# Scores of two attention heads: one fp32 product replaced by three rounded products of split queries and keys

## The reference

```python
k = rmsnorm_2(k_s, k_norm).transpose(0, 2, 1, 3)
c = jnp.cumsum(jax.nn.log_sigmoid(f_logit), axis=1).transpose(0, 2, 1)
q = rmsnorm_2(qg[..., :d].reshape(bsz, s_len, N_HEADS, HEAD_DIM), q_norm[j])
# for each block i of 128 queries:
s = jnp.einsum('bhqd,bhkd->bhqk', q_i, k, preferred_element_type=jnp.float32) * scale
s = s + c_i[..., None] - c[:, :, None, :]
s = jnp.where(kpos[None, :] <= qpos[:, None], s, -jnp.inf)
p = jax.nn.softmax(s, axis=-1)
o = jnp.einsum('bhqk,bhkd->bhqd', p.astype(v.dtype), v)
o = o * jax.nn.sigmoid(qg[..., d:])
```

## Time and profile before

| | us |
|---|---|
| median of three runs | 2042.83 |
| the three runs | 2042.83, 2043.99, 2040.23 |
| the profiled execution | 2045.83 |
| its span | 2044.0 |
| TensorE busy in the span | 2034.4 |
| VectorE, GpSimd, ScalarE busy | 963.3, 854.3, 783.7 |

### The profile page before, as it was taken

How to read it: one execution, slowest core, us unless ns; L and a number is a source line. 1 busy time by engine, 2 the same in 40 slices (tenths; PEclk the granted TensorE clock), 3 DMA queues, 4 the chain that set the end, 5 groups by cost and what they waited for, 6 DMA issues and landing times.

```text
span 2044.0 us, 24465 instructions
## 1 busy us (share of the span) xinstructions
PE 2034.4 (100%) x9826; PEld 1662.7 (81%) x9826; DVE 963.3 (47%) x1481; ACT 783.7 (38%) x1123; POOL 854.3 (42%) x357
## 2 busy tenths in 40 slices
PE   9999999999999999999999999999999999999999
PEld 7888888788888888888888888888867778888887
DVE  4588878633221314434463342444356656325242
ACT  6445656534222224512432232246256643222222
POOL 4334333544444444444444444453412234444444
PEclk9999999999999999999999999999999999999999
DMA  5222222342323222322333233232311122322333
GB/s 178 84 82 74 77 88 73 124 148 93 103 93 98 94 98 93 103 93 93 96 92 104 92 102 103 91 117 83 103 53 52 54 81 93 103 93 93 103 93 114
DMA packets 55121, 194.31 MB, mean 95 GB/s; under 512 B 6112, under 2 KB 6368, under 8 KB 55008
## 3 DMA queue, kind: packets, MB, share of 16 engines
q1 hardware_dynamic: 55008, 192.75, 29.2%
HBM read 190.62 MB, written 2.10 MB: 94 GB/s over the span
## 4 chain that ended last, share of the span: by engine, by line
PE 97%; issue 1%; DVE 1%; POOL 1%; ACT 0%; POOLq 0%; DVEq 0%
PE ps L1312 29%; PE ps L1314 29%; PE ps L1313 29%; PE ps L1626 1%; PE ps L1659 1%; PE ps L1650 1%; PE ps L1589 1%; PE ps L1591 1%; PE ps L1590 1%; PE ps L1439 1%; PE ps L1320 1%; PE ps L1341 1%; POOL w_lo L346 1%; PE ps L1366 0%; PE ps L1461 0%
## 5 line engine op out<-in xcount | busy, mean ns | idle before, releaser
L346 POOL TENSOR_TENSOR w_lo<-w_raw,w_hi 128x1024 fp32r<-128x1024 f32 x353 | 854.1, 2422 | 1177.8 <-ACT w_hi L365 1166.1
L1312 PE MATMUL ps<-a_hi,w_hi 128*128 128x512 f32 x1472 | 582.0, 395 | 1.6 <-POOL w_lo L346 1.3
L1314 PE MATMUL ps<-a_hi,w_lo 128*128 128x512 f32 x1472 | 573.9, 390 | 0.0
L1313 PE MATMUL ps<-a_lo,w_hi 128*128 128x512 f32 x1472 | 573.8, 390 | 0.0
L365 ACT CAST w_hi<-w_raw 128x1024 fp32r<-128x1024 f32 x353 | 366.2, 1041 | 324.7 <-PE ps L1314 294.4
L1312 PE MATMUL ps<-b_hi,w_hi 128*128 128x512 f32 x1176 | 459.3, 391 | 0.2 <-DVE x L787 0.2
L1314 PE MATMUL ps<-b_hi,w_lo 128*128 128x512 f32 x1176 | 457.6, 389 | 0.0
L1313 PE MATMUL ps<-b_lo,w_hi 128*128 128x512 f32 x1176 | 457.6, 389 | 0.0
L757 DVE TENSOR_TENSOR arena<-ps,inv_rms 128x512 f32<-128x512 f32 x200 | 138.0, 690 | 443.9 <-PE ps L1314 424.2
L1312 PEld LDWEIGHTS ps<-a_hi,w_hi 128*128 128x128 f32 x1472 | 276.8, 188 | 63.3 <-issue 3.2
L1313 PEld LDWEIGHTS ps<-a_lo,w_hi 128*128 128x128 f32 x1472 | 276.7, 188 | 58.6 <-issue 2.4
(11 more groups left out here) (195 smaller groups left out, 1592.9 us busy)
## 6 DMA issues: line engine op xcount, KB each, us to landing
w_raw<-in_panels SPq DMA_DIRECT2D x353, 512.0 KB, 3.5
x<-in_xT SPq DMA_DIRECT2D x16, 256.0 KB, 2.8
outT<-x SPq DMA_DIRECT2D x8, 256.0 KB, 2.0
consts<-in_const SPq DMA_DIRECT2D x1, 528.5 KB, 7.6
arena<-in_rows SPq DMA_DIRECT2D x1, 256.0 KB, 4.6
arena<-in_ws SPq DMA_DIRECT2D x1, 256.0 KB, 5.1
consts<-in_late SPq DMA_DIRECT2D x1, 168.0 KB, 2.6
params<-in_param SPq DMA_DIRECT2D x1, 116.0 KB, 2.1
```

The source lines that it names most:

```text
L346: nc.gpsimd.tensor_tensor(w_lo[:, p % RING, :], w_raw[:, p % RING, :], w_hi[:, p % RING, :].bitcast(F), ALU.subtract).then_inc(w_low, 1)
L1312: nc.tensor.matmul(o, wh, hi[:, kt, :], start=(kt == 0), stop=False)
L1313: nc.tensor.matmul(o, wh, lo[:, kt, :], start=False, stop=False)
L1314: ins = nc.tensor.matmul(o, wl, hi[:, kt, :], start=False, stop=(kt == tiles - 1))
```

## The change

The score product of a pair is no longer one fp32 product per head and block but three rounded ones: rounded query by rounded key, rounded query by rest of key, rest of query by rounded key. For this, keys and queries are split: ScalarE writes the rounded part, VectorE the rest. The split keys of pair `m` stand in tile `m` of `b_hi` and `b_lo`, where the output of the same pair will be written later; the split query stands in `sq_hi` and `sq_lo`. ScalarE splits the key of the next pair right behind the exponentials and the query behind the copies of probabilities; VectorE makes the rest of the key behind `scale_prob(a, 0)`, that of the query behind `norm_q`. Ahead of the loop both are done once for the first pair, when the last product of values has been made. `score_heads` waits for `k_low` and `q_low` instead of `q_normed`.

```diff
+        k_hi, k_lo, q_hi, q_lo = b_hi, b_lo, sq_hi, sq_lo
...
+            def split_k(a):
+                split(k_hi[:, a, :], k_all[:, a, :]).then_inc(k_high, 1)
+
+            def split_q(m):
+                act.wait_ge(q_normed, m + 1)
+                split(q_hi, q_n[:, :]).then_inc(q_high, 1)
+
+            act.wait_ge(k_normed, DT)
+            act.wait_ge(made, AT["v", DT - 1] + 1)
+            split_q(0)
+            split_k(0)
...
                 if a is not None and m is not None:
+                    split_k(m)
                     high(p + FEED)
...
                     copy_prob(a)
+                    if m is not None:
+                        split_q(m)
...
+            def rest_of_k(a):
+                dve.wait_ge(k_high, a + 1)
+                v.tensor_tensor(k_lo[:, a, :], k_all[:, a, :], k_hi[:, a, :].bitcast(F), ALU.subtract).then_inc(k_low, 1)
+
+            def rest_of_q(m):
+                dve.wait_ge(q_high, m + 1)
+                v.tensor_tensor(q_lo, q_n[:, :], q_hi.bitcast(F), ALU.subtract).then_inc(q_low, 1)
...
             take_values(1)
+            rest_of_q(0)
+            rest_of_k(0)
...
                 if a is not None and m is not None:
+                    rest_of_k(m)
                     scale_out(q_raw[:, :], p).then_inc(evicted, 1)
...
                         norm_q(m)
+                        rest_of_q(m)
                     scale_out(gate[:, m % 2, :], AT["qg", 2 * m + 1]).then_inc(evicted, 1)
...
-                pe.wait_ge(q_normed, a + 1)
+                pe.wait_ge(k_low, a + 1)
+                pe.wait_ge(q_low, a + 1)
...
-                    for side in range(2):
-                        bk, at = SCORES[side, b]
-                        nc.tensor.matmul(ps[:, bk, at:at + P * (b + 1)], q_n[half_of(side), b * P:(b + 1) * P],
-                                         k_all[half_of(side), a, 0:P * (b + 1)], start=True, stop=False)
+                    for q_part, k_part in ((q_hi, k_hi), (q_hi, k_lo), (q_lo, k_hi)):
+                        for side in range(2):
+                            bk, at = SCORES[side, b]
+                            nc.tensor.matmul(ps[:, bk, at:at + P * (b + 1)], q_part[half_of(side), b * P:(b + 1) * P],
+                                             k_part[half_of(side), a, 0:P * (b + 1)],
+                                             start=(q_part is q_hi and k_part is k_hi), stop=False)
```

More of the change, by code:

```diff
@@ L261, in build @@
         halves_made, sq_high, sq_low = sem("halves_made"), sem("sq_high"), sem("sq_low")
+        k_high, k_low, q_high, q_low = sem("k_high"), sem("k_low"), sem("q_high"), sem("q_low")
         q_squared, q_normed, gate_log, gate_arg, gate_done = (sem(n) for n in (
```

## The result

| | before | after |
|---|---|---|
| median of 19 runs each, us | 2040.37 | 2045.42 |
| most runs lie in, us | 2039.8 to 2041.0, some to 2044.0 | 2044.35 to 2045.91 |
| profiled execution, us | 2045.83 | 2044.8 |
| its span, us | 2044.0 | 2043.0 |

One run of after, at 2246.63 us with a mean granted clock of 0.851, lies apart from the other 18 and does not enter the ratio. That ratio is 1.002, interval 1.0014 to 1.0026: the change costs 2.9 to 5.3 us (the medians lie 5.05 apart). The profiled executions alone show the opposite sign, 1.0 us less after.

The account below looks back on a forecast made before the run. TensorE, with 97% of the chain, was taken to bound the kernel. First pair 0.8, middle pairs 1.0 and last pair -0.2 gave +1.6 us, forecast 2044.4 against the three-run median 2042.83; range 2038.5 to 2050.

Parts of the forecast that it names:

- first pair: First pair of heads: later weight cast and splits make TensorE wait and `low_sq` end later, +0.8 us (bounds +0.5, +1.2).
- last pair: Last pair of heads: no splits, only shorter scores, part of them lost in waits for `scale_prob`, -0.2 us.
- TensorE's saving: Score blocks of each pair: three rounded products instead of one fp32 product save 0.25 us a pair.
- Rival 3: Score blocks: weight loads are exposed, so the change isn't cheaper on TensorE; 8 x 0.9 us, 2050 us; chance 5%.
- Middle pairs: Six middle pairs: the key's split delays cast and `low_sq`, so TensorE waits; +0.17 us a pair, +1.0 us.
- One sign: Middle pairs: TensorE idle 0.3 to 0.5 us before its square sums, released by `low_sq`, would show the forecast right.
- Rival 1: Middle pairs: GpSimd's second tensor comes before `low_sq`, TensorE waits and the clock falls; 2078 us, 2060 without lower clock; 13%.
- how the profiled execution stands to the median: Base of the forecast: the profiled 2045.83 us lies 3.0 above the three-run median 2042.83, so 2047.4 becomes 2044.4.
- The start: Before the first pair's scores: splits delay the GpSimd tensor, the first key's rest ends late, TensorE waits 0.6 us.
- Rival 2: TensorE's saving comes through, 2041.9 us; second half, `low_sq` before GpSimd's second tensor in the first pair, 2037; 14% together.

Follow-up runs that it names:

- key_later: Changed kernel with the next pair's key split behind the weight cast, its rest made behind the query's norm: median 2041.32 us, ratio 0.9994 to the kernel before.
- split_twice: Changed kernel with the rounded part of the next key written twice in front of the weight cast: one execution took 2072.33 us.
- a_cast_later: Changed kernel with the pair's second weight cast only behind the split of the query: median 2042.34 us, ratio 1.0009 to the kernel before.

## Why the prediction was right, and where it was not

The time, 2045.42 us, lies in the range and 1.0 us from the forecast of 2044.4, and the change is slower, as forecast. But the change itself was forecast at +1.6 us, and the medians moved by 5.05. The close total is luck, two errors that met: the base of 2042.83, the median of three runs of which two were in the upper group, is 2.46 us above the median of 19, and the sum was 3.45 us too small. Of these, 2.25 are the first pair with its later start, 0.2 the last pair, and 1.0 lie in no trace. By the prediction's own measure of 4.1 us for what can be told from no change, the result lies on the border between "same" (72%) and "slower" (21%).

*TensorE's saving:* forecast 0.25 us a pair, measured 0.26. The blocks were forecast at 0.89, 0.59, 0.40 and 0.42 and came to 0.89, 0.58, 0.34 and 0.41. In no block is a load of 0.11 us shown except at 128 keys: the loads hide under running products on the same rows. This is against the rule that the prediction quotes from the Trainium skill, "TensorE: Matmul & The Clock Gate", section "Part 3: Packing small matmuls", that a load overlaps running products only on another row group. Rival 3 is out.

*Middle pairs:* forecast +0.17 us, measured 19.89 against 19.71 and 19.72. The split stands 0.52 us before the cast (forecast 0.54), the margin between `low_sq` and GpSimd's second tensor is 0.15 (forecast 0.13), `low_sq` keeps its turn. `key_later` and `split_twice` show the cause from both sides. One sign was off: I had named 0.3 to 0.5 us of idle time before the square sums, and 0.16 is shown. The other 0.24 us of the 0.40 lost lie in the first product behind the gap.

*Rival 1* did not happen in the middle pairs, but `split_twice` shows that it stood half a microsecond away, and its price: 24.2 us a pair where I had put 25.4. The clock was at 0.50 for 3.3 us there and for 6.7 in the traced execution of before (1498.9 to 1505.6), so the lower clock cost 1.6 us a pair, half of the 3.1 that I took.

*Last pair:* forecast -0.2, measured nothing. From its scores to the end of the program both forms take 416.2 us; the last transposes of the pair end 10.9 us after its scores begin in both. In the chain of after they stand behind `scale_prob`, so the shorter scores end in that wait, which I had put at a part only.

*First pair:* here the sum failed. I put +0.8 us, counted from the 25.62 us of the earlier trace rows, and then added it to the median of three runs. Against that form the first pair became 2.9 us shorter (22.72), since the clock did not fall in it; with the 0.8 us of the later start this is -2.1. Against the usual form, 20.57, it is +2.15 and +0.9, 3.05 where the sum has 0.8. I had seen that the profiled execution of before lay 3.0 us above the median and did not ask why. The step that failed is "how the profiled execution stands to the median": the 3 us were not an offset common to all runs, they were part of the very wait on which the term rested (5.0 us between the two traces). The start itself was right: a wait of 0.6 forecast, 0.62 measured; `low_sq` over at 1500.4 forecast, at 1500.25 measured. Held was the fourth part of `scale_prob`, not the third.

*Rival 2's* second half, in which VectorE keeps its turn in the first pair, did not occur in after, but it is how the kernel before runs in most executions, if its groups are the two forms (48 of 71). What it would have given after is shown by `a_cast_later`: 2.1 us in the first pair.

What stays open: by what the turn is decided where the distances are the same to 0.01 us, how often each form comes on a given occasion, and why the clock falls in one execution with 2.8 us of idle time and not in another with 3.0.

## What to carry to other kernels

Where a wait in a trace hangs on which of two engines gets its turn, read the trace of a second execution before a term is built on it; above all when the profiled one is off the median. And take the base from more than three runs. Cheaper products on the bounding engine give nothing if their preparation is put in front of the step that this engine waits for next: place it behind, in the idle time of its engines. And if two engines exclude each other, move the work that is not urgent (here a weight panel that is wanted a pair later) out of the other's path; on the changed kernel it gave back 2.1 us in the first pair, more than the 1.3 us that the three rounded products bring. On the kernel before no run was left in the upper group, but between the medians no gain is shown (ratio 0.9995, 0.9986 to 1.0004).

## What I had not expected of the hardware

`low_sq` on VectorE (two SBUF operands) and a GpSimd tensor take turns, and the turn is not always to the one that is ready first: at the same distance of 0.32 us `low_sq` once took 0.68 us and once 2.83. A queue of VectorE operations without a gap is not safe either: in the first pair of after the fourth part of `scale_prob`, with one SBUF operand, took 2.56 us in the midst of it, where it takes 0.47 in the same place of `a_cast_later`.

In the profiled execution of before the granted clock was already 0.50 from 1498.9 us on, in the midst of TensorE's 2.78 us of idle time, and stayed there until 1505.6. In that of after TensorE idled for 3.02 us and the clock did not fall.
